# Second feed-forward block: late forms in two pieces, three chains at once, the second half's norm moved behind the first products

## The reference, cut to what matters

```python
x = x + 0.5 * swiglu(rmsnorm(x, g_f1), w_g1, w_u1, w_d1)
x = x + mix @ w_out                       # after convolution and attention
x = x + 0.5 * swiglu(rmsnorm(x, g_f2), w_g2, w_u2, w_d2)
x = rmsnorm(x, g_fin)

def rmsnorm(x, g): return x * rsqrt(mean(x * x) + 1e-6) * g
def swiglu(x, w_gate, w_up, w_down): return (silu(x @ w_gate) * (x @ w_up)) @ w_down
# w_gate, w_up: 1024 x 2816; w_down: 2816 x 1024
```

## Time and profile before

| | us |
|---|---|
| median of 3 runs | 2103.62 (2102.03 to 2103.83) |
| the profiled execution | 2104.28 |
| its span | 2102.5 |
| PE busy | 2030.8 (97%) |
| DVE busy | 1307.0 (62%) |
| ACT busy | 991.0 (47%) |
| POOL busy | 451.3 (21%) |
| mean granted TensorE clock | 0.988 |

### The profile page before, as it was taken

The page is one execution under the profiler, slowest core; times in us unless marked ns, Lnnn a source line. Parts: engine busy times, 40 slices in busy tenths (PEclk is TensorE's granted clock), DMA queues, the critical chain, the costliest instruction groups (busy, mean ns, idle before and its releaser), DMA issues.

```text
span 2102.5 us, 35729 instructions
## 1 busy us (share of the span) xinstructions
PE 2030.8 (97%) x14062; PEld 1935.1 (92%) x14062; DVE 1307.0 (62%) x2087; ACT 991.0 (47%) x1689; POOL 451.3 (21%) x225
## 2 busy tenths in 40 slices
PE   5999999999999999999999979989999999999998
PEld 5999999999999999776877858979999999999997
DVE  7999657983425763645645664589975588723323
ACT  6556344564334431455555652265543456433423
POOL 0000000004666643011012332000000000166662
PEclk8999999999999999999999989999999999999999
DMA  7554324555755447321122133055432265485742
GB/s 230 135 145 132 92 63 143 164 150 186 240 181 188 136 133 51 89 77 46 53 77 54 48 137 130 1 174 160 134 102 82 85 182 162 128 274 173 236 140 113
DMA packets 296853, 274.52 MB, mean 131 GB/s; under 512 B 29864, under 2 KB 238888, under 8 KB 296432
## 3 DMA queue, kind: packets, MB, share of 16 engines
q1 hardware_dynamic: 296688, 272.25, 43.5%
HBM read 222.41 MB, written 49.80 MB: 129 GB/s over the span
## 4 chain that ended last, share of the span: by engine, by line
PE 88%; DVE 5%; ACT 4%; issue 1%; another core or an unknown queue 0%; DVEq 0%; ACTq 0%
PE banks L277 27%; PE banks L278 27%; PE banks L279 26%; PE banks L2766 3%; DVE scores_minusF L2208 1%; PE banks L2734 1%; PE banks L2735 1%; PE banks L2688 1%; ACT k_hi_twice L1400 1%; PE banks L3016 0%; DVE head_rstd L1710 0%; DVE head_rstd L1706 0%; DVE head_rstd L1708 0%; ACT head_r L1088 0%
## 5 line engine op out<-in xcount | busy, mean ns | idle before, releaser
L277 PE MATMUL banks<-hforms_hi,w_hi 128*128 128x264 f32 x2112 | 602.6, 285 | 18.5 <-DVE hforms_lo L1910 9.6
L278 PE MATMUL banks<-hforms_lo,w_hi 128*128 128x264 f32 x2112 | 602.9, 285 | 0.0
L279 PE MATMUL banks<-hforms_hi,w_lo 128*128 128x264 f32 x2112 | 601.5, 285 | 0.0
L968 POOL TENSOR_TENSOR w_lo<-w_raw,w_hi 128x1024 fp32r<-128x1024 f32 x132 | 321.9, 2443 | 1203.2 <-ACT w_hi L1196 1203.2
L277 PEld LDWEIGHTS banks<-hforms_hi,w_hi 128*128 128x128 f32 x2112 | 399.5, 189 | 22.1 <-issue 7.2
L279 PEld LDWEIGHTS banks<-hforms_hi,w_lo 128*128 128x128 f32 x2112 | 398.9, 189 | 0.0
L278 PEld LDWEIGHTS banks<-hforms_lo,w_hi 128*128 128x128 f32 x2112 | 398.5, 189 | 0.1
L277 PE MATMUL banks<-acts_a,w_hi 128*128 128x352 f32 x960 | 309.9, 323 | 0.0
L279 PE MATMUL banks<-acts_a,w_lo 128*128 128x352 f32 x960 | 309.2, 322 | 0.0
L278 PE MATMUL banks<-acts_a,w_hi 128*128 128x352 f32 x960 | 309.0, 322 | 0.0
L1196 ACT ACTIVATE w_hi<-w_raw 128x1024 fp32r<-128x1024 f32 x132 | 139.5, 1058 | 283.1 <-PE banks L279 259.3
(11 more groups left out here) (338 smaller groups left out, 3557.4 us busy)
## 6 DMA issues: line engine op xcount, KB each, us to landing
w_raw<-in_w_ffn_down SPq DMA_DIRECT2D x132, 512.0 KB, 3.8
w_raw<-in_w_ffn_gate SPq DMA_DIRECT2D x76, 512.0 KB, 5.4
w_raw<-in_w_ffn_up SPq DMA_DIRECT2D x76, 512.0 KB, 5.2
act_rows<-act_f SPq DMA_DIRECT2D x44, 528.0 KB, 2.9
acts_f<-act_rows SPq DMA_DIRECT2D x66, 352.0 KB, 4.1
w_raw<-in_w_in SPq DMA_DIRECT2D x20, 512.0 KB, 5.7
x_spill<-xT SPq DMA_DIRECT2D x4, 2112.0 KB, 8.5
xT<-x_spill SPq DMA_DIRECT2D x6, 1408.0 KB, 9.3
```

Source lines behind the costliest of these rows:

```text
L277: eng.matmul(out, w_hi, x_hi, start=first, stop=False, skip_group_check=added)
L278: eng.matmul(out, w_hi, x_lo, start=False, stop=False, skip_group_check=added)
L279: return eng.matmul(out, w_lo, x_hi, start=False, stop=last, skip_group_check=added)
L968: pool.tensor_tensor(wlo[:, wd_slot(e), :], raw[:, wd_slot(e), :], whi[:, wd_slot(e), :].bitcast(F32), ALU.subtract)\
```

## The change

All of it is in the second block (`n` = 1) but for the counting of semaphores. (a) The high and low forms of kk = 2 and 3 are each made in two pieces, q 0 to 3 and q 4 to 6, and counted by `forms_count`. (b) On ACT the weight parts 3 and 4 and the load of the silu table go ahead of these forms, and on DVE the low weight parts 1 and 2 ahead of the last residual, and `sums_lo` 1 between the pieces. (c) PE begins product 0 with q0, q2 and q3 for kk 0 and 1, then q0 and q2 for kk 2 and 3, q1, the rest of q3, and on. (d) The squares of the second half go to products 0 and 1 (ACT), the half sums to products 1 and 2 (DVE), the means (behind q1) and the roots to product 3, with one load of each table around the rough roots. (e) The second half's forms move from products 2, 6, 10, 14 to 4, 8, 11, 14, their low parts from 4, 8, 12, 16 to 6, 10, 13, 16.

```diff
-        FORMS_AT = [4 * kk + 2 for kk in range(4)]
-        FORMS_LO_AT = [4 * kk + 4 for kk in range(4)]
+        FORMS_AT = [[2, 6, 10, 14], [4, 8, 11, 14]]
+        FORMS_LO_AT = [[w + 2 for w in at] for at in FORMS_AT]
+        SQUARES_AT, HALVES_AT, ROOTS_AT = [0, 1], [1, 2], 3
+        def forms_count(n, z, kk, q):
+            m = 8 * n + 4 * z + kk
+            if n and (z, kk) in ((0, 2), (0, 3)):
+                return 2 * (8 * n + 2) + kk - 1 + (2 if q > 4 else 0)
+            if n and (z, kk) in ((1, -2), (1, -1)):
+                return 2 * (8 * n + 4)
+            return 2 * (m + 1)
...
 # ACT, ahead of the products
                 if n:
-                    part_hi("gate", u0, 2)
-                    forms_hi(n, 0, 2)
-                    forms_hi(n, 0, 3)
-                    half_squares(n, 2, ready)
-                    half_squares(n, 3, ready)
-                    part_hi("gate", u0, 3)
+                    for part in (2, 3, 4):
+                        part_hi("gate", u0, part)
+                    nc.scalar.preload_act_table_set(SILU_SET)
+                    for qs in ((0, 4), (4, 7)):
+                        forms_hi(n, 0, 2, qs)
+                        forms_hi(n, 0, 3, qs)
...
 # ACT, in a product
                     if nxt and first:
                         part_hi(*nxt, 1)
+                    if n and w in SQUARES_AT:
+                        half_squares(n, 2 + SQUARES_AT.index(w), ready)
+                    if n and w == ROOTS_AT:
+                        nc.scalar.preload_act_table_set(EXP_LN_SET)
+                        half_rough(n, 2)
+                        half_rough(n, 3)
+                        nc.scalar.preload_act_table_set(SILU_SET)
...
-                    if n and w == 1:
-                        nc.scalar.preload_act_table_set(EXP_LN_SET)
-                        half_rough(n, 2)
-                        half_rough(n, 3)
-                        nc.scalar.preload_act_table_set(SILU_SET)
...
 # DVE, ahead of the products
-                    out_resid(2 * KT + 5, 3 * KT)
-                    forms_lo(n, 0, 2)
-                    forms_lo(n, 0, 3)
+                    out_resid(2 * KT + 5, 3 * KT - 1)
+                    part_lo("gate", u0, 1)
+                    part_lo("gate", u0, 2)
+                    out_resid(3 * KT - 1, 3 * KT)
+                    forms_lo(n, 0, 2, (0, 4))
+                    forms_lo(n, 0, 3, (0, 4))
+                    sums_lo("gate", u0, 1)
+                    forms_lo(n, 0, 2, (4, 7))
+                    forms_lo(n, 0, 3, (4, 7))
...
 # DVE, in a product
-                    if n and w == 0:
-                        half_sums(n, 2)
-                        half_sums(n, 3)
-                    if w == n:
+                    if n and w in HALVES_AT:
+                        half_sums(n, 2 + HALVES_AT.index(w))
+                    if w == (ROOTS_AT if n else 0):
                         half_rstd(n, 2)
                         half_rstd(n, 3)
...
 # PE, the first product
-                if by_block:
+                if by_block and n:
+                    for q in (0, 2, 3):
+                        ready(q)
+                    for kk in range(2):
+                        for q in (0, 2, 3):
+                            part(q, kk)
+                    for kk in (2, 3):
+                        for q in (0, 2):
+                            part(q, kk)
+                    ready(1)
+                    for kk in range(4):
+                        part(1, kk)
+                    for kk in (2, 3):
+                        part(3, kk)
+                elif by_block:
...
-                    if means and q == ORDER[4]:
+                    if means and q == ORDER[2]:
                         half_mean_of_sum(n, 2)
                         half_mean_of_sum(n, 3)
...
-                    pair_product(n, which, u, s, z, b0, w == 0, n and w == 1)
+                    pair_product(n, which, u, s, z, b0, w == 0, n and w == ROOTS_AT)
```

More of the change, by code:

```diff
@@ L654, in load_acts @@
                 elif p == 0:
-                    sp.wait_ge(FFN["forms_lo"], 8 * n + 8)
+                    sp.wait_ge(FFN["forms_lo"], 2 * (8 * n + 8))
                 sp.dma_start(astg[:, m % 4, :, :],
@@ L1151, in silu, with forms_hi @@
                     act.activation(gq[:, s % 2, q, :], gq[:, s % 2, q, :], ACT.Silu).then_inc(f["silu"], 1)
-            def forms_hi(n, z, kk):
+            def forms_hi(n, z, kk, qs=(0, 7)):
                 f = FFN
@@ L1161, in forms_hi @@
                     act.wait_ge(OUT["done"], 3 * KT if kk else 2 * KT)
-                act.activation(HH[z][:, :, kk, :], FT[:, m % 2, 0:7, :], ACT.Copy).then_inc(f["forms_hi"], 1)
+                r = slice(*qs)
+                act.activation(HH[z][:, r, kk, :], FT[:, m % 2, r, :], ACT.Copy)\
+                    .then_inc(f["forms_hi"], 2 if qs == (0, 7) else 1)
             def half_squares(n, c, ready):
@@ L1247, in ffn @@
                     forms_hi(n, 0, 3)
-                more_free()
-                part_hi("gate", u0, 4)
-                if n == 0:
+                    more_free()
+                    part_hi("gate", u0, 4)
                     half_rough(n, 2)
                     half_rough(n, 3)
-                nc.scalar.preload_act_table_set(SILU_SET)
+                    nc.scalar.preload_act_table_set(SILU_SET)
                 gate_before = None
@@ L1267, in ffn @@
                     copy(which, s, b0, 2)
-                    if w - 1 in FORMS_AT:
-                        forms_hi(n, 1, FORMS_AT.index(w - 1))
+                    if w - 1 in FORMS_AT[n]:
+                        forms_hi(n, 1, FORMS_AT[n].index(w - 1))
                     if nxt and first:
                         part_hi(*nxt, 1)
+                    if n and w in SQUARES_AT:
[4 more added lines that the diff above has]
+                        half_rough(n, 3)
+                        nc.scalar.preload_act_table_set(SILU_SET)
                     if 0 <= w - ACTS_AT < NF - 1:
@@ L1871, in forms_normed @@
                     if m >= 2:
-                        dve.wait_ge(f["forms_hi"], m - 1)
-                        dve.wait_ge(f["forms_lo"], m - 1)
+                        dve.wait_ge(f["forms_hi"], forms_count(n, z, kk - 2, 7) if z or kk >= 2 else 2 * (m - 1))
+                        dve.wait_ge(f["forms_lo"], forms_count(n, z, kk - 2, 7) if z or kk >= 2 else 2 * (m - 1))
                     dve.wait_ge(FNORM["dve"], 12 * n + 6 * z + 6)
@@ L1907, in forms_lo @@
                 m = 8 * n + 4 * z + kk
-                dve.wait_ge(f["forms_hi"], m + 1)
+                dve.wait_ge(f["forms_hi"], forms_count(n, z, kk, qs[1]))
                 r = slice(*qs)
                 lo = dve.tensor_tensor(HL[z][:, r, kk, :], FT[:, m % 2, r, :], HH[z][:, r, kk, :].bitcast(F32), ALU.subtract)
-                if qs[1] == 7:
+                if n and z == 0 and kk >= 2:
                     lo.then_inc(f["forms_lo"], 1)
+                elif qs[1] == 7:
+                    lo.then_inc(f["forms_lo"], 2)
             def out_resid(m0, m1):
@@ L2000, in ffn @@
                     nxt = next_run(which, u)
-                    if first:
+                    if first and not (n and w == 0):
                         part_lo(which, u, 1)
@@ L2012, in ffn @@
                         act_lo(n, 0, w - ACTS_AT)
[L2013 to L2016, removed]
+                    if w in FORMS_LO_AT[n]:
+                        forms_lo(n, 1, FORMS_LO_AT[n].index(w), (0, 3))
+                    if w in FORMS_AT[n]:
+                        forms_normed(n, 1, FORMS_AT[n].index(w), 0)
                     combine(which, s, b0, 1)
[L2018 to L2021, removed]
+                    if w in FORMS_LO_AT[n]:
+                        forms_lo(n, 1, FORMS_LO_AT[n].index(w), (3, 7))
+                    if w in FORMS_AT[n]:
+                        forms_normed(n, 1, FORMS_AT[n].index(w), 1)
                     if which == "up":
@@ L2032, in ffn @@
                         multiply(s, b0, 2)
-                    if n and w == 0:
-                        half_sums(n, 2)
-                        half_sums(n, 3)
-                    if w == n:
+                    if n and w in HALVES_AT:
+                        half_sums(n, 2 + HALVES_AT.index(w))
+                    if w == (ROOTS_AT if n else 0):
                         half_rstd(n, 2)
                         half_rstd(n, 3)
-                    if w in FORMS_AT:
-                        forms_sums(n, 1, FORMS_AT.index(w), 0)
-                        forms_sums(n, 1, FORMS_AT.index(w), 1)
+                    if w in FORMS_AT[n]:
+                        forms_sums(n, 1, FORMS_AT[n].index(w), 0)
+                        forms_sums(n, 1, FORMS_AT[n].index(w), 1)
                 act_lo(n, 0, NF - 1)
@@ L2460, in part @@
                     w_hi, w_lo = slots(whi, wxh, G[q], 1), slots(wlo, wxl, G[q], 1)
-                    pe.wait_ge(f["forms_lo"], 8 * n + 4 * z + kk + 1)
```

(3 more changed lines are left out.)

## The result

The changed kernel takes 2105.97 us (median of 16 runs, 2103.09 to 2109.33) against 2102.03 for the kernel before (16 runs on the same chip): a ratio of 1.0020, 95% interval 1.0013 to 1.0026. It is slower by 3.9 us (2.7 to 5.5), where 2.6 us of gain were forecast, and it lies outside the range. The profiled execution took 2106.59 us (span 2104.8, granted clock 0.989); it reached product 0 1.88 us earlier than the one before. That is not put down to the change: the start of product 0 lies between 1361.3 and 1365.4 in the nine profiled executions, and at 1361.30 in one whose program up to there is that of before.

The account below looks back on a forecast made before the run. TensorE, busy 97%, was taken as the bound, with only some 11 us of gaps to win. Product steps left 3.1 us, DVE's budget 1.9; gain 2.6 from 2104.28, less 0.66, gave 2101.0 us, range 2096.0 to 2105.6.

Parts of the forecast that it names:

- Product 0: Start of the second block: forms in pieces and three chains end it at 1376.4 instead of 1384.1, gain 7.7 us.
- Product 1: Pair 1's gate weights land at 1384.5, PE waits 2.9 us plus 1.5 of low clock; gain left 5.1.
- mark 3: First matmul on `w_more_hi` in product 3, read against the kernel before: 9.0 us of gain predicted left there.
- Products 2 to 4: Gain left 9.0 us after product 2, 8.1 with the means in product 3, 6.4 after late copy, forms and combine.
- price of a table load: On ACT, 1.28 us by the trace row, next instruction 0.01 later, kept against the skill page's 2.66 per switch.
- SP in products 4 and 8: SP's reload waits for a same-product form, delaying gate weights; PE waits 2.0 and 1.3 us in products 5 and 9.
- T + 7.4: Predicted landing of gate weights in products 4 and 8; T is the end of that form's second multiplication.
- the rival that was given 0.12: SP's new order is slower: weights behind a reload take 10.3 us instead of 6.1, giving 2111.9; chance 0.12.
- once x is back, DMA is half idle: Argument against the slower SP-order rival, in which weights behind a reload take 10.3 us instead of 6.1.
- DVE's budget: Check from 1365.3 to product 15's end: gain at most 12.3 less new DVE waits of 10.4, leaving 1.9 us.
- some 11: Microseconds of PE waits and low clock in the edited stretch, 0.5% of the time, taken to bound the gain.
- the dearer table load: Skill page's 2.66 us per switch: product 3's two loads cost 2.76 more, sum near 2103.9; chance 0.03.

Follow-up runs that it names:

- reload behind: Changed kernel with SP issuing each second-block reload of x behind the next pair's gate weights instead of ahead: 2099.53 us, ratio 0.9986.
- weights first: Changed kernel with SP issuing the gate weights of pair 1 ahead of the two spills of x: 2099.12 us, ratio 0.9991.
- both: Changed kernel with reloads behind the next gate weights and pair 1's gate weights ahead of the spills: 2093.14 us, ratio 0.9956.
- places alone: Kernel before with only the second half's forms moved to products 4, 8, 11, 14, SP's reload and wait going along: 2110.76 us, ratio 1.0040.
- places with the reload behind: Kernel before with second-half forms at 4, 8, 11, 14 and SP's reload and its wait behind the next gate weights: 2104.44 us, ratio 1.0009.
- copies first: Changed kernel with ACT's high piece of gate pair 1 behind the second and third PSUM copies in product 1: 2106.42 us, ratio 1.0017.

## Why the prediction was wrong

The step that failed is the landing of the gate weights, in product 1 and behind the forms of products 4 and 8: the prediction had the queues and the waits, took the landings too early, and so the waits too short (2.9 and 2.0 us, measured 4.29 and 3.39) and the low clock behind them too cheap (1.5 us and nothing, measured 2.5 and 1.4).

**Product 0: right.** 7.8 us for 7.7. q1 starts at 1367.69, which is 1369.57 in the time of before (1369.7 was forecast), and PE keeps its full clock (granted 1.00 from 1363.5 to 1377).

**Product 1: the mechanism right, two sizes off.** The weights of pair 1 take the place of what was removed, and hold ACT's piece until 1383.92, 1385.8 in the time of before; 1384.5 was taken, 1385.5 was the end of the range. SP did issue them earlier relative to product 0 (8.1 us after its start, not 9.4), and it gave nothing: they landed 10.4 and 10.9 us later instead of 7.8 and 10.3, the last of them 20.4 us after the start of product 0, where it was 20.2 before. So PE waited 4.29, not 2.9. Behind it 25 matmuls start 0.22 us apart, not 15: 2.5 us instead of 1.5. Windows of after (stretch, length, busy time of PE, PEld, DVE, ACT, POOL, granted clock, DMA):
```profile
1385.10:1388.60 3.50, 3.40 (x15) 3.43 (x16) 2.49 (x6) 2.76 (x3) 0.00 (x0) 0.50 0.06 14
1388.60:1391.90 3.30, 3.30 (x20) 3.30 (x19) 2.02 (x6) 1.66 (x3) 0.00 (x0) 0.62 0.00 0
```
Together these are 2.4 us, beside the 2.3 that mark 3 stands short of the forecast.

**Products 2 to 4: right.** 2.6 us were to go between marks 3 and 5, and 2.7 went: ACT's copy behind the table loads (0.68), the combine (0.62), the means. The price of a table load, which the prediction took from the row, holds again: 1.28 us at 1411.01, and the next ACT instruction 0.02 later. No load stands around the squares at 1372.25. The Trainium skill ("ScalarE: Activation LUTs", section "What ACT_TABLE_LOAD costs") states some 2.66 us for a switch, a drain included; the trace of after, as that of before, shows the load alone.

**SP in products 4 and 8: the step that failed.** The prediction had the new order and the wait, and put the weights' landing at T + 7.4. They landed at 1434.2, T + 9.05. The second issue comes 1.36 after T, not 1.0, and it takes 7.7 us to land, not 6.4. The prediction had taken 0.3, of a bound of 1.3, for the 528 KB reload just ahead of the weights, on top of the 6.1 of the earlier trace rows. That load stood behind a reload too, but one issued 1.9 us ahead of it in the kernel before:
```profile
1423.69 0.58 SPq L645 DMA_DIRECT2D x_again<-x_spill  x1
```
In the changed kernel the reload is issued 0.67 us ahead of the weights, and the second of the two takes 1.6 us longer to land; with the reload behind them it took 5.3. So PE waited 3.39 us instead of 2.0, and that was enough for what the prediction had priced only as a bound, the lower clock:
```profile
1435.40:1438.90 3.50, 3.41 (x15) 3.44 (x16) 2.48 (x6) 3.09 (x3) 0.00 (x0) 0.51 0.22 54
1438.90:1442.30 3.40, 3.40 (x30) 3.40 (x29) 3.04 (x6) 1.61 (x2) 0.00 (x0) 1.00 0.00 0
```
Fourteen matmuls start 0.22 us apart there, 1.4 us, and by the second window the clock is back at full. The form in product 4 cost 5.2 us (in product 5) instead of 2.0, the one in product 8 cost 1.8 instead of 1.3. This is the rival that was given 0.12, in a milder form (its 10.3 us was from a load that stood behind both spills as well as a reload): it named the point from which it turns to a loss, 1.6 us later on each load, and in product 4 the landing is 1.65 later. What spoke against it ("once x is back, DMA is half idle") is true and beside the point: DMA is 0.33 busy from 1396 to 1425, but the reload itself stands ahead of the weights, and from 1427 to 1431 the share is 0.98 or more. The run with the reload behind gets 6.4 us back.

**DVE's budget: the waits too small, and not a bound.** 12.3 less DVE's new waits was to bound the gain. The new waits sum to 17.4 us, not 10.4 (10.8 alone for gate weights), and 12.3 - 17.4 = -5.1 stands beside the -4.3 of the marks. That is near, but the gain exceeds its bound, and so it does with the reload behind, with the weights first and with both, by 0.8 to 1.4 (both: 12.3 - 4.4 = 7.9, marks 9.3).

**Not foreseen: products 11 to 14, 1.3 us.** The forms at 11 come back as two small steps of PE in product 12 (0.3 us), their low half at 13 as two in product 14 (1.0 us), the last of them the 0.29 at 1527.68 for `w_lo`. The steps are there in every kernel with these places, also where no other wait is left (10.6 to 9.3 in the table). The places tell more: an odd product is an `up` product, in which DVE has the multiplications as well. With all places even (the kernel before) the steps are absent. With 4, 7, 10, 13 they follow the forms at 7 and 13 and the low halves at 9 and 15, and none follows an even place. Those of product 16 stand there with no form in product 16, so the next form is not what makes them. That places in `up` products are the cause is read from the nine traces; the runs moved several places at a time, and none has the whole change with even places only.

Of the 7.4 us between forecast and marks (3.1 and -4.3), 2.3 are product 1, 3.2 product 4, 0.5 product 8 and 1.3 the `up` places, 7.3 together. The forecast was lower than 3.1 by the budget, which was wrong in the same terms.

Three figures of the prediction do not add up, without weight for the forecast: the waits and low clock to be won are 12.8 us (9.8 and 3.0), not some 11; the work that ACT does early is 4.8 us by its own list, not 3.6 (its end, 1363.9, is that of 4.8); and by the dearer table load the sum would end at 2103.8, not 2103.9.

Open: what sets how long the clock stays low after a wait, and whether it falls at all (last section).

## What to carry to other kernels

When work is moved to a later place, look first at the queues that issue loads in order: a wait that was long over at the old place can be live at the new one, and it then delays every load behind it. Here that order cost 6.7 us in the kernel before, and with the load ahead of the wait the changed kernel was 2.5 us faster than the one before, not 3.9 slower. And a predicted wait that comes within a microsecond of one after which the clock fell should be priced with a share of that clock too: in these products of the nine traces it fell after every wait of PE of 2.4 us or more but one.

## What the runs showed of the hardware that was not expected

- Issuing the gate weights 1.4 us earlier behind the same 4.2 MB of spills did not make them land earlier: 10.4 and 10.9 us instead of 7.8 and 10.3. Their place ahead of the spills did: they landed 4.1 and 5.4 us after their issue in the run with the weights first.
- The stretch at the low clock was not of one length, and the wait ahead of it does not tell it. After the waits of 2.4 to 3.5 us 12 to 18 matmuls started 0.22 us apart; three kernels that are the same up to there (before, places alone, places with the reload behind) had 14, 18 and 12 after the wait of 3.4, 3.4 and 3.2 us in product 0. There were 25 and 21 after those of 4.29 and 4.30 us in product 1 (after, and reload behind), but 13 after one of 4.04 us and none after one of 3.49 us (both copies first).
